# A chunked RWKV-7 recurrence: inverting all chunks in three groups ahead of the steps, instead of ten ahead and seven between the steps

## The reference, cut to what matters

```python
def _wkv_step(S, inp):
    r_t, w_t, k_t, v_t, a_t, b_t = inp
    sa = jnp.einsum('bhvk,bhk->bhv', S, a_t)
    S = S * w_t[:, :, None, :] + sa[..., None] * b_t[:, :, None, :] + v_t[..., None] * k_t[:, :, None, :]
    y = jnp.einsum('bhvk,bhk->bhv', S, r_t)
    return S, y
...
    S_fin, ys = lax.scan(_wkv_step, wkv_state.astype(jnp.float32), xs)
```

## Time and profile before

| | |
|---|---|
| time, median of three runs | 2093.12 us (2091.69 to 2096.31) |
| the profiled execution's own time | 2095.49 us |
| its span | 2093.5 us |
| PE (TensorE matmul) busy | 1763.4 us, 84% |
| DVE busy | 666.8 us, 32% |
| ACT busy | 427.4 us, 20% |
| granted PE clock, mean over the span | 0.907 |

### The profile page before, as it was taken

How to read it: one execution, slowest core, us unless ns; L and a number is a source line. 1 busy time by engine, 2 the same in 40 slices (tenths; PEclk the granted TensorE clock), 3 DMA queues, 4 the chain that set the end, 5 groups by cost and what they waited for, 6 DMA issues and landing times. The chain is left out here.

```text
span 2093.5 us, 35714 instructions
## 1 busy us (share of the span) xinstructions
PE 1763.4 (84%) x15376; PEld 1256.3 (60%) x15376; DVE 666.8 (32%) x1533; ACT 427.4 (20%) x852; POOL 71.9 (3%) x76
## 2 busy tenths in 40 slices
PE   3597987999799696979797979988399999991897
PEld 2266855865686585747575755436178888880443
DVE  3125434425443442141424242124211111114233
ACT  2121131123013111040404041002101111112233
POOL 0000000000000000000000000000300000004000
PEclk7797998999899797999999988998799999996899
DMA  3001001000100100332323252006269999975210
GB/s 123 20 19 31 3 13 31 3 14 1 32 3 13 31 3 33 165 142 106 148 105 149 101 208 81 0 19 265 105 227 364 365 368 363 365 267 201 102 40 35
DMA packets 74542, 244.15 MB, mean 117 GB/s; under 512 B 13712, under 2 KB 36496, under 8 KB 64656
## 3 DMA queue, kind: packets, MB, share of 16 engines
q1 hardware_dynamic: 62000, 198.82, 25.8%
q0 software_dynamic: 7776, 26.23, 3.4%
q10 hardware_dynamic: 4608, 16.78, 2.0%
HBM read 210.00 MB, written 31.81 MB: 116 GB/s over the span
## 5 line engine op out<-in xcount | busy, mean ns | idle before, releaser
L387 PE MATMUL bank<-h,w 128*128 128x352 f32 (+1 forms) x576 | 184.1, 477 | 26.9 <-PEq L274 26.9
L387 PEld LDWEIGHTS bank<-h,w 128*128 128x128 f32 x576 | 110.0, 194 | 94.2 <-issue 31.7
L1751 DVE COPY xgT<-bank 128x512 f32<-128x512 f32 x64 | 41.2, 686 | 319.2 <-PE bank L1683 319.2
L1697 PEld LDWEIGHTS bank<-xgT,we_g 128*128 128x128 f32 x1024 | 121.5, 195 | 17.7 <-issue 14.3
L971 PE MATMUL bank<-h,wqkv 128*128 128x352 f32 (+1 forms) x384 | 120.8, 477 | 13.1 <-DMA wqkv<-in_wqkv 13.1
L1893 PE MATMUL bank<-wp,unT 128*128 128x512 f32 (+1 forms) x288 | 127.0, 600 | 0.0
L1697 PE MATMUL bank<-xgT,we_g 128*128 128x128 f32 x1024 | 122.0, 278 | 2.8 <-DVE xgT L1751 2.8
L1697 PE MATMUL bank<-xgT,we_u 128*128 128x128 f32 x1024 | 119.6, 275 | 0.0
L1697 PEld LDWEIGHTS bank<-xgT,we_u 128*128 128x128 f32 x1024 | 116.9, 192 | 0.0
L1707 PE MATMUL bank<-we_d,hT 128*128 128x512 f32 x256 | 115.0, 592 | 0.0
L971 PEld LDWEIGHTS bank<-h,wqkv 128*128 128x128 f32 x384 | 74.2, 194 | 57.6 <-issue 15.7
(11 more groups left out here) (363 smaller groups left out, 2722.4 us busy)
## 6 DMA issues: line engine op xcount, KB each, us to landing
we_g<-in_weg SPq DMA_DIRECT2D x32, 1024.0 KB, 5.9
we_u<-in_weu SPq DMA_DIRECT2D x32, 1024.0 KB, 9.5
we_d<-in_wed SPq DMA_DIRECT2D x32, 1024.0 KB, 12.1
cache<-in_kcj SPq DMA_DIRECT2D x4, 5120.0 KB, 16.3
cache<-in_vcj SPq DMA_DIRECT2D x4, 5120.0 KB, 15.7
y_rows<-yo ACTq DMA_DIRECT2D x32, 512.0 KB
w<-in_win SPq DMA_DIRECT2D x15, 512.0 KB, 6.1
wqkv<-in_wqkv SPq DMA_DIRECT2D x4, 1536.0 KB, 18.9
```

Source lines behind the costliest of these rows:

```text
L387: mm = pe.matmul(out, w3[:, kd, q, :], g.uT[:, kd, a:a + w], start=(kd == 0), stop=(kd == KD - 1))
L1697: mm = pe.matmul(bank[2 + e % 2][:, 128 * (2 * a + f):128 * (2 * a + f) + CAP], w[:, k, 128 * f:128 * f + 128], xT[e % 2][:, k, :], start= ...
L1751: last = dve.tensor_copy(xT[e % 2][:, 4 * c:4 * c + 4, :].rearrange("p k q -> p (k q)"), bank[c][:, :])
```

## The change: one group of 17 chunks in three subgroups, all before the steps

`SUBS` becomes (0-5, 6-11, 12-16), each with two banks of its own (`ZB`, `XB`; banks 2 to 7). There are 14 hops of three parts, 42 parts in all, and all stand ahead of the first step. The other products use banks 0 and 1 only. They come in 13 pairs, one behind the first part of each hop: `bk` by `ar` for both heads in turn, or both transposes, or two of the pieces of turned `ar` and value products. A pair waits until both banks have been read (`b_free0`, `b_free1`), and the first pair waits for nothing. All state products and the sample states' products follow, and then 17 steps with no inversion between them.

```diff
-            SUBS = [[(0, 5), (5, 5)], [(10, 4), (14, 3)]]
-            FIRST = 10
-            PARTS = 28
-            BV = [(0, 8, 22), (8, 8, 23), (16, 1, 26)]
-            AT = [(0, 8, 21), (8, 8, 25)]
-            WT = [(0, 5, 6), (5, 5, 7), (10, 6, 4)]
+            SUBS = [(0, 6), (6, 6), (12, 5)]
+            ZB, XB = (2, 4, 6), (3, 5, 7)
+            HOPS = 14
+            PARTS = 3 * HOPS
+            PIECES = [(0, 6), (6, 6), (12, 5)]
+            PAIRS = 13
+            kind_of = lambda k: ("z", "x", "t")[k // 3 % 3]
+            pair_after = lambda k: k // 3 if k % 3 == 0 and k // 3 < PAIRS else None
...
+                    def job_pair(n):
+
+                        if n:
+                            pe.wait_ge(s["b_free0"], n)
+                            pe.wait_ge(s["b_free1"], n)
+                        if n < 10:
+                            q = n // 2
+                            for c in range(4 * q, min(4 * q + 4, NCH)):
+                                o = slice(128 * (c - 4 * q), 128 * (c - 4 * q) + 128)
+                                if n % 2 == 0:
+                                    for hh in range(2):
+                                        mm = pe.matmul(bank[hh][:, o], bk[hs(hh), c, :, :], ar[hs(hh), c, :, :], start=True, stop=True)
+                                else:
+                                    pe.transpose(bank[0][:, o], both(bk[:, c, :, :]), g.ident[:, :])
+                            if n % 2:
+                                for c in range(4 * q, min(4 * q + 4, NCH)):
+                                    o = slice(128 * (c - 4 * q), 128 * (c - 4 * q) + 128)
+                                    mm = pe.matmul(bank[1][64:128, o], v[:, c * CW:c * CW + CW], g.ident[:, :], start=True, stop=True)
+                            mm.then_inc(s["b_job"], 2)
+                            return
...
-                    for step in range(PARTS):
-                        inverse_part(0, step)
-                        if step < 20:
-                            if step == 0:
-                                pe.wait_ge(s["b_init"], 4)
-                            pair_products(step // 4, step % 4)
...
-                    for c in range(FIRST):
-                        if c == 5:
-                            pe.wait_ge(s["c_wtev"], 2)
-                        step_u(c)
-                        if 3 * c < PARTS:
-                            inverse_part(1, 3 * c)
-                        if 3 * c + 1 < PARTS:
-                            inverse_part(1, 3 * c + 1)
-                        step_state(c)
-                        if 3 * c + 2 < PARTS:
-                            inverse_part(1, 3 * c + 2)
-                    pe.wait_ge(s["b_xev"], 20)
-                    state_products(2)
-
+                    for k in range(PARTS):
+                        inverse_part(k)
+                        if pair_after(k) is not None:
+                            job_pair(pair_after(k))
+                    pe.wait_ge(s["b_xev"], 3 * 5)
+                    pe.wait_ge(s["b_free0"], PAIRS)
+                    pe.wait_ge(s["b_free1"], PAIRS)
+                    for i in range(3):
+                        state_products(i)
...
-                    for c in range(FIRST, NCH):
+                    for c in range(NCH):
                         step_u(c)
-                        if c == FIRST + 1:
+                        if c == 1:
...
+                    for k in range(PARTS):
+                        inverse_out(k)
+                        n = pair_after(k)
+                        if n is not None and n < 10 and n % 2 == 0:
+                            q = n // 2
                             c0, c1 = 4 * q, min(4 * q + 4, NCH)
+                            dve.wait_ge(s["b_job"], 2 * n + 2)
+                            for hh in range(2):
+                                dve.tensor_tensor(gm[:, c0:c1, hh, :], bank[hh][:, 0:128 * (c1 - c0)].rearrange("p (c x) -> p c x", c=c1 - c0),
+                                                  br(g.m_pair[:, 0 if c1 <= NC else 1, :], c1 - c0), ALU.mult).then_inc(free[hh], 1)
```

More of the change, by code:

```diff
@@ L524, in recur_pair @@
             SC = slice(448, 512)
+            free = (s["b_free0"], s["b_free1"])
+            turned_piece = lambda n: (PIECES[n][0], min(PIECES[n][1], NC - PIECES[n][0]))
             with nc.Block() as block:
@@ L552, in inverse_part @@
                                 else:
-                                    mm = pe.matmul(bank[4 + sub][hs(hh), o:o + CW], zb[hs(hh), c, :], xb[hs(hh), c, :], start=True, stop=True)
+                                    mm = pe.matmul(bank[ZB[sub]][hs(hh), o:o + CW], zb[hs(hh), c, :], xb[hs(hh), c, :], start=True, stop=True)
                         mm.then_inc(s["b_" + kind], 1)
[L556 to L560, removed]
-                            else:
[L562 to L571, removed]
@@ L694, in _ @@
                 def _(act):
[L695 to L703, removed]
@@ L716, in _ @@
-                    turned(0)
-                    values(0)
-                    values(1)
-                    turned(1)
-                    values(2)
-                    products(0)
-                    products(1)
+                    for n in range(1, 10, 2):
+                        q = n // 2
+                        c0, c1 = 4 * q, min(4 * q + 4, NCH)
+                        act.wait_ge(s["b_job"], 2 * n + 2)
+                        act.activation(bkt[:, c0:c1, :, :].rearrange("p c h e -> p (c h e)"), bank[0][:, 0:128 * (c1 - c0)], ACT.Copy).then_inc(free[0], 1)
+                        act.activation(uv[64:128, c0:c1, :, :].rearrange("p c h e -> p (c h e)"), bank[1][64:128, 0:128 * (c1 - c0)], ACT.Copy).then_inc(free[1], 1)
@@ new lines, in _ @@
+                    for x in range(20, 26):
+                        c0, m = turned_piece(x - 20) if x < 23 else PIECES[x - 23]
+                        act.wait_ge(s["b_job"], x + 1)
+                        act.activation((wt if x < 23 else bv)[:, c0:c0 + m, :], bank[x % 2][:, 0:m * CW].rearrange("p (c x) -> p c x", c=m), ACT.Copy).then_inc(free[x % 2], 1)
+                    for i in range(3):
+                        c0, m = turned_piece(i)
+                        act.wait_ge(s["c_wt"], i + 1)
+                        act.activation(wt[:, c0:c0 + m, :], bank[ZB[i]][:, 0:m * CW].rearrange("p (c x) -> p c x", c=m), ACT.Copy).then_inc(s["c_wtev"], 1)
@@ new lines, in _ @@
+                    for c in range(NCH):
+                        dve.wait_ge(s["c_u"], c + 1)
+                        dve.tensor_copy(uv[0:64, c, 1, :], bank[1][0:64, 0:E]).then_inc(s["c_uev1"], 1)
+                        if c < NC:
+                            dve.wait_ge(s["c_s"], c + 1)
+                            if c >= 1:
+                                dve.wait_ge(s["c_y"], c)
+                            dve.tensor_scalar(st[:, (c + 1) % 2, :], sbank(c)[:, SC], gat(c), None, ALU.mult).then_inc(s["c_sev"], 1)
```

145 lines of the change are left out of this document (46 added, 99 removed).

## The result

The changed kernel takes 2071.05 us in the median of four runs (2069.47 to 2073.77), the kernel before 2094.72 on the same chip. The ratio is 0.9887 [0.9865, 0.9909], so the change gains 1.1%. The forecast of 2066 us is near, but part of that is luck, as the windows show.

A forecast was written before the change was run, and what follows sets the result against it. The prediction saw one long chain, TensorE bounding most of each recurrence and latency the bare steps. Terms summed to 82.0 us against 88.4 in the second recurrence, 29.4 gained over four, 2 added for a start's clock: 2066 us, range 2056 to 2084.

The forecast's parts named there:

- Start: From the first inversion part to the second pair of jobs: 5.8 us, or 6.8 in the third and fourth recurrence.
- The low clock: Rival: TensorE stays at 1.2 GHz at the start of the inversions, 12.5 us over four recurrences, 2078 us; chance 0.15.
- Even pairs: Pairs of other products with both heads in turn: 1.15 us for 16 records, 3.5 for pairs 2, 4 and 6.
- the heads don't overlap: Rival: the even pairs' heads run one after the other, 2.0 us for 16 records, 11.8 in all, 2078; chance 0.12.
- The reading of the L1016 row: Attention's 8 records of 512 columns in 1.91 us, heads in turn, were taken to show heads running side by side.
- Ahead of the steps: All stages from the first inversion part to the first step: about 51 us in the second recurrence.
- the inversion and its returns: Ahead of the steps: 215 chunks at 30.5 ns a record, 26.2 us, and nine returns from wide products, 1.0 us.
- Steps: The 17 steps with no inversion between them: 12.8 us for the last seven, 17.8 for the others, 30.6 in all.
- the steps alone lose the full clock: Rival: bare steps fall to 1.2 GHz, 1.1 us longer each; ten slow in four recurrences cost 44 us, 2110; chance 0.09.
- signs of being wrong: L568 at 2.0 us, PEclk under 0.9 in steps, idle before L570 every other hop, recurrences not falling to about 88.
- The price of the change: Group 1's 392 records cost 7.9 us between the steps and 12.0 ahead of them: 4.1 us more in each recurrence.
- The total: Second recurrence 82.0 us against 88.4; four recurrences gain 29.4; 2 us added for one low-clock start: 2066 us.

The follow-up runs named there:

- e2: The changed kernel with four more 64x64 matmuls (8 records) per step into a bank nobody reads, while PE waits for u: 2049.39 us, ratio 0.9803.
- e6: e2 with the first pair's old wait on all of DVE's initialisations put back: 2058.56 us, ratio 0.9874.
- e3: The changed kernel with all of head 0's records before head 1's in the even pairs: 2078.8 us, ratio 0.9939.
- e4: The changed kernel with two groups inverted ahead and the third (chunks 12 to 16) between the matmuls of the first twelve steps: 2036.44 us, ratio 0.9736.
- e8: e7 with groups of 7, 7 and 3 chunks, the last group's parts one in each of fourteen steps: 2031.61 us, ratio 0.9748.
- e1: The changed kernel with the carried state in a bank of its own, moving the wait for the copy of y off the path: 2068.39 us, ratio 0.9909.
- e9: The changed kernel again, unaltered, on another chip: 2077.25 us, ratio 0.9923.
- e5: e2 with all of head 0's records before head 1's in the even pairs: 2053.96 us, ratio 0.9852.
- e7: e4 with the state summed in the single bank of e1: 2040.86 us, ratio 0.9787.
- e10: e4 once more, on another chip: 2031.42 us, ratio 0.9723.
- e12: e8 with the states in bank 5, so only the first copy of the state products is awaited before the steps: 2027.3 us, ratio 0.9726.

## Why the prediction was right, and where it wasn't

- *Start.* Right: 5.8 us until the second pair of jobs were forecast, 5.4 measured (359.95 to L570 at 365.39). The low clock stays away in two recurrences and comes for 3.4 us in each of the other two: over the first 12.85 us the granted clock is 0.87, 1.00, 0.87 and 1.00, against 0.63 to 0.73 over the first eight blocks before. The prediction had put 2 us on one such start, and there were two; the stage ahead was 204.1 us, against 201.0 in e2, where all four starts were clean. e6 sizes the wait with its clock at 8.8 us.
- *Even pairs.* Right: 1.15 us forecast, 1.09 measured. The rival (the heads don't overlap, 2.0 us) is refuted by the 1.09 itself, and e3, where the order alone makes it 1.64, shows that the order does it. The reading of the L1016 row carried over. The Trainium skill (TensorEngine Tiling (Array Packing), Key Properties) says that tiles execute in parallel; e3 against the changed kernel agrees, with the addition that the order of issue decides how much of it is had.
- *Ahead of the steps.* 51.4 us forecast from first part to first step, 49.75 measured in the second recurrence; over all four some 207.6 against 201.0 in e2. The terms were each somewhat high: start 0.4, even pairs 0.06 each, and the rest is in the inversion and its returns (the 44 records from 370.19 to 371.52 take 30.2 ns each). Which of these holds the last microsecond wasn't measured apart.
- *Steps.* 30.6 us forecast, 30.57 measured, wherever the clock held. That it would hold was the step that failed. The prediction gave "the steps alone lose the full clock" 0.09 and argued that it had held in all of the alone stretch until step 16. But that stretch was 12.3 us long, and the steps alone last 30; in the changed kernel one recurrence fell only behind the 10th L625. A stretch that holds for seven steps doesn't speak for seventeen. The sign was there to be read: in the kernel before, the clock fell 0.5 to 1.5 us ahead of the end of all four alone stretches, in the first recurrence 11.6 us behind its start:

```profile
271.37:272.84 1.47, 1.47 (x9) 1.00 (x9) 1.17 (x2) 0.00 (x0) 0.00 (x0) 0.50 0.03 6
```

  The price was mis-sized as well: a slow step costs 0.8 us more and not 1.1. The prediction had multiplied all 1.45 us of PE's busy time by what a row of parts showed, 1.26 against 0.72. In a step PE is busy for 2.31 us in place of 1.42, less than that factor, and its idle time falls from 0.33 to 0.20. DVE (0.50) and ACT (0.22) don't change. So the rival came true in part: 19.5 us in place of 44 over four recurrences, which takes two thirds of the forecast gain of 29.4 and doesn't turn it. Two of the prediction's own signs of being wrong came true: PEclk was 0.75, 0.64 and 0.72 in the steps of three recurrences, and these three took 92.9 to 96.5 us where about 88 were forecast. The Trainium skill (TensorE: Matmul & The Clock Gate, A second HAM failure mode: psum-queue depth-cycling) warned of short idle times between groups of matmuls; e2 and the 12 of 16 agree with it here, with the difference that the clock didn't oscillate but stayed low to the recurrence's end.
- *The price of the change.* "In each recurrence 4.1 us, since group 1 is no longer hidden" was right in kind. e4 undoes it for five chunks (before, it was seven) while keeping the new start and pairs. Against e2, where the clock holds as well, its recurrences are 331.1 us in place of 347.8, which is 4.2 us each; that it is the forecast's 4.1 almost to the digit is chance, the numbers of chunks and of steps being others. Against the changed kernel itself e4 and e8 win 1.5 and 1.4% (0.9736 and 0.9748 against 0.9887). In the traces e4's recurrences are 38.5 us shorter, and 19.5 us of that, half, is the clock in the steps.
- *The total.* Recurrences gained 14.2 us where 27.4 were forecast (29.4 less 2). From the 29.4: the clock in the steps took 19.5, the stage ahead was 3.5 better than forecast (204.1 against 207.6), and the A products 0.7 shorter than before. A further 7.3 us of the span came from code that the change doesn't touch, and that is the luck in the forecast's nearness. Had the clock held in the steps and at the starts, as in e2, the recurrences would sum to 347.8 in place of 383.8 us, and the time would be about 2093 - 36 = 2057 us by this estimate, at the low end of the forecast's range. e2's ratio of 0.9803 gives 2052, below it, but holds some us of the untouched code too.

Left open: what exactly makes the clock fall at one step and not at another. It fell behind the 5th to the 14th L625, from 8.2 to 25 us after the first matmul of the steps, with and without the pause. Nor was it tried whether fewer than 8 fill records would do.

## What to carry to other kernels

- Work that hides in the idle times of a latency-bound loop does two things: it costs less there than elsewhere (12 records free, 20 records for 0.2 us instead of 0.6 where a step has one such part), and it keeps TensorE's clock up. Before moving it out, price both.
- If a loop must run bare, put a few matmuls that nobody reads where PE waits anyway, and read the granted clock loop by loop. A clock that held over a short stretch before is no evidence for a longer one.
- A forecast that lands near the time isn't yet right. Sum the stages that the change touches and those that it doesn't.

## What the runs showed of the hardware

- TensorE can lose its full clock with PE shown busy for 9.16 of 10.89 us (the third recurrence's steps up to the fall), and keep it with PE busy for 25.07 of 30.57 (the second recurrence's). Between these two the busy share of the records is no guide to whether the clock holds. With 8 short records more a step (28.98 of 30.58) it held in 12 of 12.
- Once down in the steps, it stayed down to the end of the recurrence, for as much as 31.9 us, with PE shown busy for 29.2 of them (e3, third recurrence):

```profile
583.28:615.20 31.92, 29.19 (x293) 22.29 (x290) 7.29 (x26) 3.41 (x15) 0.00 (x0) 0.50 0.01 2
```

- Two heads' matmuls on different rows (0 to 63 and 64 to 127) and banks, 16 records of 128 columns: 1.09 us in turn, 1.64 one head after the other.
- The spread goes with the clock: kernels with bare steps ranged over 20 to 27 us within their runs (e1, e3 without its one slowest, e9; the changed kernel's first four runs over 4), those with fill over 5 to 7 us (e2, e5, e6) and those with parts over 6 to 13 (e4, e7, e8, e10 to e12).
